# Router weights held still, tokens split straight from the sum banks, and three steps moved, in a two-layer transformer kernel

## What is computed

```python
x = layer_norm(DEEPNORM_ALPHA * x + gate[:, None, :] * y, ln_g[layer, 0], ln_b[layer, 0])
h = modulate(x, shift, scale)
y = moe_ffn(h, ...)
x = layer_norm(DEEPNORM_ALPHA * x + gate[:, None, :] * y, ln_g[layer, 1], ln_b[layer, 1])

def route(x2, w_router, b_router):            # x2: 256 tokens x 1024
    probs = jax.nn.softmax((x2 @ w_router).astype(jnp.float32), axis=-1)     # 16 experts
    sel_scores = (probs + b_router).reshape(T, N_GROUPS, EXPERTS_PER_GROUP)
    grp_score = lax.top_k(sel_scores, MOE_TOPK)[0].sum(-1)
    g = jnp.argmax(grp_score, axis=-1)        # one group of 4, then the 2 best experts in it
    ...
# each token's two experts: (silu(x @ w_gate) * (x @ w_up)) @ w_down, weighted and added
```

## Time and profile before

| | before |
|---|---|
| median of 3 runs | 2516.6 us |
| profiled execution, own time | 2522.8 us |
| its span, first to last instruction | 2521.1 us |
| TensorE busy / VectorE / ScalarE / Pool | 92% / 49% / 37% / 5% |
| chain that ended last: TensorE / VectorE / ScalarE | 82% / 10% / 3% |
| mean granted TensorE clock | 0.961 |
| HBM read | 532.81 MB, 212 GB/s over the span |

### The profile page before, as it was taken

The page is one execution under the profiler, slowest core; times in us unless marked ns, Lnnn a source line. Parts: engine busy times, 40 slices in busy tenths (PEclk is TensorE's granted clock), DMA queues, the critical chain, the costliest instruction groups (busy, mean ns, idle before and its releaser), DMA issues.

```text
span 2521.1 us, 33462 instructions
## 1 busy us (share of the span) xinstructions
PE 2324.4 (92%) x13002; PEld 1784.3 (71%) x13002; DVE 1238.6 (49%) x2282; ACT 941.7 (37%) x1668; POOL 124.0 (5%) x104
## 2 busy tenths in 40 slices
PE   6999998898889889977999989999999999899999
PEld 4875587444457644436888769988878886698887
DVE  4522334211132421116773746677777736666776
ACT  3432212111032311106544455464454445545553
POOL 1000000000000000000003400000000042000000
PEclk9999998899999889998998999999999999899999
DMA  9858845599911569993653413556656634045562
GB/s 327 316 184 296 300 188 200 246 427 428 400 67 67 234 259 427 427 353 100 197 182 118 167 67 135 172 171 184 198 157 194 185 120 167 34 168 167 176 199 92
DMA packets 306465, 535.68 MB, mean 212 GB/s; under 512 B 12639, under 2 KB 198689, under 8 KB 294049
## 3 DMA queue, kind: packets, MB, share of 16 engines
q1 hardware_dynamic: 305388, 532.61, 58.8%
q10 hardware_dynamic: 948, 1.28, 0.2%
HBM read 532.81 MB, written 1.05 MB: 212 GB/s over the span
## 4 chain that ended last, share of the span: by engine, by line
PE 82%; DVE 10%; ACT 3%; issue 2%; DMA 2%; SPq 0%; DVEq 0%; ACTq 0%
PE bank L578 15%; PE bank L982 14%; PE bank L844 12%; PE yacc L878 9%; PE bank L849 6%; PE bank L562 4%; PE yacc L774 2%; PE bank L613 2%; PE yacc L595 2%; PE bank L1196 1%; PE bank L940 1%; PE bank L642 1%; PE yacc L1140 1%; PE yacc L994 1%; PE bank L1110 1%
## 5 line engine op out<-in xcount | busy, mean ns | idle before, releaser
L1359 ACT ACTIVATE arena<-bank 128x256 f32<-128x256 f32 (+3 forms) x390 | 152.2, 411 | 623.2 <-PE bank L578 125.5
L844 PE MATMUL bank<-h_split,w_hi 128*128 128x512 f32 x1408 | 351.5, 392 | 0.0
L2176 DVE TENSOR_TENSOR w_lo<-wring,w_hi 128x1024 fp32r<-128x1024 f32 x264 | 307.5, 1219 | 10.8 <-ACT w_hi L1544 10.7
L1544 ACT ACTIVATE w_hi<-wring 128x1024 fp32r<-128x1024 f32 x264 | 277.4, 1056 | 49.0 <-PE yacc L878 49.0
L844 PEld LDWEIGHTS bank<-h_split,w_hi 128*128 128x128 f32 x1408 | 259.0, 189 | 49.8
L982 PE MATMUL bank<-wring,arena 128*64 128x512 f32 x896 | 241.9, 602 | 17.9 <-issue 14.4
L849 PEld LDWEIGHTS bank<-h_split,w_lo 128*128 128x128 f32 x1408 | 193.7, 192 | 18.6 <-DVE h_split L2218 4.1
L849 PE MATMUL bank<-h_split,w_lo 128*128 128x256 f32 x1408 | 199.6, 285 | 3.8 <-DVE h_split L2218 3.8
L982 PE MATMUL bank<-arena 128*64 128x512 f32 x640 | 185.9, 605 | 11.2 <-issue 7.2
L982 PEld LDWEIGHTS bank<-wring,arena 128*64 128x64 f32 x896 | 86.0, 138 | 133.0 <-issue 133.0
L2732 POOL TENSOR_TENSOR wx_lo<-wring,wx_hi 128x1024 fp32r<-128x1024 f32 x42 | 107.6, 2563 | 1154.8 <-ACT wx_hi L1399 1154.8
(11 more groups left out here) (395 smaller groups left out, 3837.3 us busy)
## 6 DMA issues: line engine op xcount, KB each, us to landing
wring<-in_ffn_w_in SPq DMA_DIRECT2D x176, 512.0 KB
wring<-in_w_ada SPq DMA_DIRECT2D x28, 2048.0 KB
wring<-in_ffn_w_out SPq DMA_DIRECT2D x88, 512.0 KB
wring<-in_moe_w_gate SPq DMA_DIRECT2D x20, 2048.0 KB, 20.6
wring<-in_moe_w_up SPq DMA_DIRECT2D x20, 2048.0 KB, 16.9
wring<-in_w_in SPq DMA_DIRECT2D x20, 2048.0 KB
arena<-in_moe_w_down SPq DMA_DIRECT2D x16, 2048.0 KB, 19.5
wring<-in_moe_w_down SPq DMA_DIRECT2D x16, 2048.0 KB, 19.0
```

Of the source, the lines that this page charges most:

```text
L844: return mm(b[:, :], r(w_hi[:, j % 2, g, c * HB:(c + 1) * HB]), r(h_split[:, c, :, :].rearrange("p a t -> p (a t)")), start=start, stop=st ...
L1359: ins = f(dst, bank_of(name)[0:dst.shape[0], 0:T] if src is None else src, func, **kw)
L1544: f(w_hi[:, j % 2, part, :].bitcast(F32R), wring[:, u % WSLOTS, part * DC * HB:(part + 1) * DC * HB], ACT.Copy).then_inc(w_hi_ready[part], 1)
L2176: tt(w_lo[:, j % 2, part, :].bitcast(F32R), wring[:, (u0 + j) % WSLOTS, part * DC * HB:(part + 1) * DC * HB], w_hi[:, j % 2, part, :], ALU ...
```

## The change

It has four parts, the same in both layers.

1. *Router product.* The router's weights are now stationary (128x16) and H moves, 256 columns at a time: eight products into a 16x256 result. VectorE copies that to `nrm`, and two small transposes turn it into 128x32 for the tokens.
2. *Tokens.* The transposes of H are woven between the first four products and put behind the last, and go to the sum banks yacc. ScalarE rounds them into tok_hi, one copy each instead of two. VectorE takes over Pool's subtraction and reads yacc directly (`tokens_low`): one bank before it reads the ranks, three behind fill_slots. The first gather does all high products first, into all four banks, and then the low ones.
3. *Residual and angles.* `layer_norm` hands back the scaling of X as a function; it and the angles run on VectorE in the first pair, before the product of gate and up.
4. *Flag.* The wait and the load stand at pair 4 on TensorE, ScalarE, VectorE and SyncE; the branch stays at the end.

```diff
@@ TensorE, routing
+                def turn_tokens(k):
+                    for i in range(TT):
+                        last = nc.tensor.transpose(yacc[TT * (k // 4) + i][:, (k % 4) * P:(k % 4 + 1) * P],
+                                                   H[:, k, i * P:(i + 1) * P], ident[:, :])
+                        if k % 4 == 3:
+                            last.then_inc(tok_turned, 1)
                 b = fill(f"logits{l}")
+                for k in range(DC):
+                    pe.wait_ge(h_ready.sem, h_ready.upto("pe"))
+                    last = mm(b[0:NE, 0:T], wr[:, k, :], H[:, k, :], start=(k == 0), stop=(k == DC - 1))
+                    if k < 4:
+                        turn_tokens(k)
+                filled(f"logits{l}", last)
+                for k in range(4, DC):
+                    turn_tokens(k)
+                pe.wait_ge(*drained(f"logits{l}"))
+                b = fill(f"logT{l}")
                 for i in range(TT):
-                    for k in range(DC):
-                        if i == 0:
-                            pe.wait_ge(h_ready.sem, h_ready.upto("pe"))
-                        last = mm(b[:, i * NE:(i + 1) * NE], H[:, k, i * P:(i + 1) * P], wr[:, k, :],
-                                  start=(k == 0), stop=(k == DC - 1))
-                filled(f"logits{l}", last)
-                for n in range(2 * TT):
...
+                    last = nc.tensor.transpose(b[:, i * NE:(i + 1) * NE], nrm[0:NE, 1, i * P:(i + 1) * P], ident[0:NE, 0:NE])
+                filled(f"logT{l}", last)
@@ TensorE, gather
+                    if q == 0:
+                        for k in range(DC):
+                            if k % 2 == 0:
+                                fill(f"moe{l}.xg{q}.{k // 2}")
+                            tile(k, 0, tok_hi)
...
+                            if k == 0:
+                                pe.wait_ge(tok_lowered, 2 * TT * (l + 1))
...
+                        last = tile(k, 1, tok_lo)
@@ TensorE, moe (ScalarE, VectorE and SyncE alike)
+                    if p == PAIRS // 2:
+                        pe.wait_ge(flagged, l + 1)
+                        flag = pe.value_load(over_flag[0:1, l:l + 1], min_val=0, max_val=1)
                     if p:
                         scatter(p - 1)
...
-                pe.wait_ge(flagged, l + 1)
-                flag = pe.value_load(over_flag[0:1, l:l + 1], min_val=0, max_val=1)
                 with pe.If(flag > 0):
@@ ScalarE, routing
-                    evac(f"ht{l}.{n}", Htok[:, i, :, half_row], b, last=False)
-                    evac(f"ht{l}.{n}", tok_hi[:, i, :, half_row].bitcast(F32R), b)
+                    act.wait_ge(tok_turned, 2 * TT * l + n + 1)
+                    f(tok_hi[:, i, :, half * (P // 2):(half + 1) * (P // 2)].bitcast(F32R),
+                      yacc[n][:, :].rearrange("p (c k) -> p k c", k=DC), ACT.Copy).then_inc(tok_split, 1)
@@ VectorE
+            def tokens_low(l, n):
...
+                tt(tok_lo[:, i, :, half_row].bitcast(F32R), yacc[n][:, :].rearrange("p (c k) -> p k c", k=DC),
+                   tok_hi[:, i, :, half_row], ALU.subtract).then_inc(tok_lowered, 1)
@@ VectorE, routing
+                moved(f"logits{l}", v.tensor_copy(nrm[0:NE, 1, :], bank_of(f"logits{l}")[0:NE, 0:T]))
+                dve.wait_ge(*full(f"logT{l}"))
...
+                tokens_low(l, 0)
                 dve.wait_ge(*full(f"rank{l}"))
@@ VectorE, moe
                 fill_slots(l, 0)
+                for n in range(1, 2 * TT):
+                    tokens_low(l, n)
                 weigh_slots(l, 0)
...
+                    if p == 0:
+                        later()
@@ Pool
-                    g.tensor_tensor(tok_lo[:, i, :, half_row].bitcast(F32R), Htok[:, i, :, half_row],
-                                    tok_hi[:, i, :, half_row], ALU.subtract).then_inc(tok_split, 1)
```

More of the change, by code:

```diff
@@ L450, in build @@
         XG = view(0, DC, 2 * P)
-        Htok = view(0, TT, DC, P)
         slot_g = view(2048, TT, 2, SLOTS)
@@ L956, in turn_slots @@
                     filled(f"moe{l}.S{p}", last)
-                for n in range(2 * TT):
-                    pe.wait_ge(*drained(f"ht{l}.{n}"))
                 pe.wait_ge(tok_split, 2 * TT * (l + 1))
```

90 lines of the change are left out of this document (48 added, 42 removed).

## The result

| us | kernel before | changed kernel |
|---|---|---|
| median (lowest to highest) of 5 runs | 2516.8 (2515.94 to 2524.29) | **2504.13** (2498.62 to 2505.21) |
| ratio, 95% interval | 1 | 0.994, 0.9922 to 0.9958 |
| span of the profiled execution | 2521.1 | 2502.4 |

The changed kernel is faster by 12.7 us between the medians; 2506.6 was forecast, 2501.5 to 2512.5 as the range. The two profiled spans differ by more, 18.7 us.

A forecast was written before the change was run, and what follows sets the result against it. The prediction took VectorE's routing chain, then the weights' transfers, to set the pace around the experts; its terms summed to -10.0 us, taken with the profile's 6.2 us offset to 2506.6 us, range 2501.5 to 2512.5.

The forecast's parts named there:

- Pool leaves: Routing, both layers: VectorE's small additions, held up during Pool's subtractions, return to usual speed; -7.6 us.
- subtraction: VectorE before the ranks: the first subtraction mostly fits a 0.76 us wait; +0.4 us for both layers.
- Angles: Layer 0, between reading the ranks and the slots: angles move behind TensorE's first expert products; -2.7 us.
- Logits: Router, first logit product to read: new product with woven transposes, priced between full and half clock; +0.6 us, both layers.
- Gather split: First gather, both layers: TensorE may wait after the high products for three more subtractions; +0.6 us.
- Flag: End of the experts, both layers: load and register steps leave TensorE's queue, so the branch begins 0.65 earlier; -1.3 us.
- Moves the whole stage: Experts, once per layer: each microsecond the first product starts earlier moves the weight-paced stage, and the gain reaches the end.
- Pool is innocent: Rival, routing: the slow additions come from something that stays, so 7.6 us go; 2514.2 us, chance 0.06.
- the branch's wait goes too: Rival, end of experts: the moved code's target is at hand, up to 5 us more per layer; 2496 to 2502, chance 0.06.
- Full clock: Rival, router: the denser product brings the clock up at once, -4.0 instead of +0.6; 2502.0 us, chance 0.15.
- Half clock throughout: Rival, router: clock stays at half through the logits, +8.2 instead of +0.6; 2514.2 us, chance 0.08.
- The slower side: Rival, ranks to experts: VectorE's subtractions aren't hidden, gain gone from 2.2 us each; 2523.6 us at 3.1, chance 0.03.

The follow-up runs named there:

- 12: Changed kernel with the tokens' low parts back on Pool, ScalarE copying for it and VectorE's four subtractions left out: 2511.46 us, ratio to before 0.9982.
- 2: Kernel before with one wait more, so that Pool starts its four subtractions only when the experts are chosen: 2517.32 us, ratio 0.999.
- 4: Changed kernel with the rotary angles back between the routing and the first slots, in layer 0 only: 2506.86 us.
- 11: Changed kernel with the first gather in the old order, high and low parts of a chunk together: 2508.64 us, ratio 0.9958.
- 1: Kernel before with only the flag's wait and reading moved to the middle pair, the branch staying at the end: 2516.36 us, ratio 0.9991.
- 6: Changed kernel with the slot-overflow code as one loop over 64 blocks, TensorE's jump passing some 175 instructions instead of 465: 2488.58 us, ratio to before 0.9873.

## Why the prediction was right

The forecast of 2506.6 missed the median by 2.5 us, and its sum of -10.0 is what the two stages of the profiles gave. The large terms, Pool and angles, were right in mechanism and size. That the sum agrees to 0.1 is luck: the other parts missed by up to 1.5 us, with either sign. By its own steps:

- **Pool leaves (-7.6) and subtraction (+0.4).** Right. Read to slots fell by 3.75 in layer 1, where only one subtraction was added there. It cost nothing: 0.69 in a wait of 0.76. 12 and 2 show the cause.
- **Angles (-2.7).** Right: 6.47 less in layer 0 against 3.75 in layer 1, and 4 gives 2.7 back.
- **Logits (+0.6).** Measured +1.2. "If the clock comes up 3 us after the start" didn't hold: it began full, fell after 1.3 and 1.7 us and came back 4.7 and 5.1 us after the start, in layers 0 and 1. The term was sized too low by 0.3 per layer, and it hid a loss: with the residual gone the old product reads at 8.1, so against that the new one costs 1.3 per layer. I had read the residual's wait (0.7) and not counted it as a gain of its own. And of the sixteen transposes, which the prediction calls woven, eight are; eight stand behind the last product.
- **Gather split (+0.6).** Measured +0.4. Without the split the first expert product is 2.1 to 2.6 later (11): the part earns its place only because the low parts moved to VectorE.
- **Flag (-1.3).** Measured -1.6 in the change and -1.5 alone (1). The branch starts 0.84 sooner after the scatter in layer 0: the load's 0.65 and, by what is left, a short time ahead of it.
- **"Moves the whole stage", and nothing after it.** Not quite, and one of the prediction's signs of being wrong came: in layer 0, where the start was won by 5.3, 1.7 came back before the last scatter. The traces say where. Over the two layers of the fourteen profiled executions this stretch took 221.2 to 222.1 us in thirteen cases and 222.8 to 223.8 in fifteen. In the fifteen, and in no other, the granted clock falls to 0.50 some 202 to 203 us after the first expert product, at the start of the last up product, behind which no wait for weights is left that could take the loss up; falls elsewhere in the stretch come in both groups. The rows stand under 11. No edit lies inside it; why the fall comes there isn't shown. In layer 1, where it came before and after, the start won 3.3 and the last scatter 3.5. There the mean's products gained 1.3, at a clock of 0.71 in place of 0.56. The two cancelled in the sum; that part of the agreement is luck.
- **The rest of the gain.** What goes beyond 10 lies in code that wasn't touched, by the granted clock. The prediction put nothing there, and why the clock was higher behind the change isn't settled.
- **Rivals.** "Pool is innocent" is refuted, "the branch's wait goes too" didn't happen, though 6 shows that it can. "Full clock" came true in one layer of some executions, but its price was off: by rows of products and transposes alone it had 5.6 us to the read, and at the full clock throughout the read came 6.79 us after the first product (4), a gain of 0.85 per layer in place of 2.0. "Half clock throughout" (11.7) was never seen; the latest read came 9.26 after the first product. The slower side needed reads of 2.2 us; they took 0.68 to 0.69.

The largest loss in this stretch was one I had read and left: the branch. The short code of 6 gives 2488.6, 15.6 below the changed kernel and 1.3% below the one before.

## What to carry to other kernels

When small VectorE operations take a multiple of their usual time, look at what Pool does in those microseconds; take the work away from Pool rather than moving it, since the slowness goes where Pool goes. A rarely taken piece of code can cost by the length of the jump over it, even when it is never entered (here 6.2 to 7.0 us against 0.2 to 0.4): read the branch row, and try such code as a loop. Judge an edit of one or two microseconds by its stage in the profile, between landmarks around it, and expect it to be hidden where the clock gives or takes as much further on (1.7 us in the experts here, 1.3 in the mean). Work that waits for the same thing as its neighbour is worth little until the neighbour is fast: the residual cost 0.1 beside the router's product at a falling clock and 1.6 beside it at the full one.

## What the runs showed of the hardware

- TensorE's jump over some 465 instructions (a count from the code) took 6.15 to 6.96 us in every execution; over some 175, 0.21 to 0.41. The same branches on ScalarE and VectorE, over shorter code, took 0.05 to 0.07. Where between the two lengths the cost begins wasn't tried.
- Pool holds up more than the additions: beside it a cast of 128x2 took 0.83 us (0.17 before) and two scalings 2.41 (0.37 before), each ending within 0.05 us of the end of one of Pool's four subtractions, which take 1.27 us each, while a reduction and a reciprocal beside it kept 0.19 and 0.17.
- The same 16 passes of 256 columns with 16-column weights took 3.61, 5.30 and 6.28 us in different places and executions, at granted clocks between 1.00 and 0.56. What sets the level at the start of such a stretch isn't shown.
- VectorE's strided reads of a bank into an fp32r tile of 128x512 took 0.68 to 0.69 us each, three in a row 1.88, no more than the contiguous ones (0.69).
